# Order of the eight experts in a mixture-of-experts stage, few-row and many-row experts placed differently

## What is computed

```
logits = (tokens @ router_w)
top_vals, top_idx = lax.top_k(logits, 2)
gates = softmax(top_vals)
# for each of the 8 experts e, over the tokens routed to it:
y = (silu(xb @ w1[e]) * (xb @ w3[e])) @ w2[e]      # 1024 -> 2816 -> 1024
out[token] += gate * y
```

## Time and profile before

| what | value |
|---|---|
| median of 3 runs | 2088.28 us (2087.71 to 2107.45) |
| the profiled execution's own time | 2087.27 us |
| its span, first to last instruction | 2084.3 us |
| TensorE matmul busy | 1908.1 us (92%) |
| VectorE, ScalarE busy | 830.7 us (40%), 393.8 us (19%) |
| weight stream | 450 loads of 1 MB, 6.9 us median from issue to landing |

### The profile page before, as it was taken

The page is one execution under the profiler, slowest core; times in us unless marked ns, Lnnn a source line. Parts: engine busy times, 40 slices in busy tenths (PEclk is TensorE's granted clock), DMA queues, the critical chain, the costliest instruction groups (busy, mean ns, idle before and its releaser), DMA issues. The chain is left out here.

```text
span 2084.3 us, 46584 instructions
## 1 busy us (share of the span) xinstructions
PE 1908.1 (92%) x19815; PEld 1617.2 (78%) x19815; DVE 830.7 (40%) x2260; ACT 393.8 (19%) x1114; POOL 0.5 (0%) x5
## 2 busy tenths in 40 slices
PE   6999897999979886999999999999979998899987
PEld 4677676888878776986989968999757876778766
DVE  3856542777758712011101111010113676126651
ACT  2332332000014131000001000000002233122331
POOL 0000000000000000000000000000000000000000
PEclk8999997999989876999999999999998999899988
DMA  9523241889863121989998999989893412234100
GB/s 391 218 101 121 93 171 67 338 335 350 340 245 123 40 81 55 376 330 420 419 349 340 351 392 419 388 321 384 348 419 122 188 73 81 81 121 162 41 1 20
DMA packets 67922, 480.38 MB, mean 230 GB/s; under 512 B 7424, under 2 KB 9728, under 8 KB 9856
## 3 DMA queue, kind: packets, MB, share of 16 engines
q1 hardware_dynamic: 67712, 477.36, 59.2%
HBM read 476.28 MB, written 1.05 MB: 229 GB/s over the span
## 5 line engine op out<-in xcount | busy, mean ns | idle before, releaser
L441 PE MATMUL PS<-sb_U,sb_ring 128*128 128x256 f32 (+1 forms) x1456 | 371.2, 412 | 19.2 <-PEq L217 12.8
L441 PEld LDWEIGHTS PS<-sb_U,sb_ring 128*128 128x128 f32 x1456 | 279.4, 195 | 96.0 <-issue 60.4
L1612 PE MATMUL PS<-sb_arena,sb_ring 128*64 128x98 f32 x7040 | 305.5, 247 | 10.0 <-issue 7.8
L1612 PEld LDWEIGHTS PS<-sb_arena,sb_ring 128*64 128x64 f32 x7040 | 299.5, 136 | 17.0 <-issue 13.3
L688 PE MATMUL PS<-sb_U,sb_ring 128*128 128x256 f32 x704 | 159.6, 386 | 5.7 <-PEq L217 5.7
L1628 PE MATMUL PS<-sb_arena,sb_ring 128*64 128x98 f32 x3520 | 156.6, 248 | 1.6 <-issue 1.4
L1628 PEld LDWEIGHTS PS<-sb_arena,sb_ring 128*64 128x64 f32 x3520 | 149.8, 137 | 9.6 <-ACT sb_arena L1893 6.6
L441 PE MATMUL PS<-sb_arena 128*64 128x128 f32 (+9 forms) x884 | 149.5, 343 | 7.2 <-DVE sb_arena L652 4.4
L688 PEld LDWEIGHTS PS<-sb_U,sb_ring 128*128 128x128 f32 x704 | 134.2, 193 | 23.9 <-issue 6.0
L1945 DVE TENSOR_TENSOR sb_arena<-PS,sb_arena 128x98 f32<-128x98 f32 x110 | 28.6, 260 | 291.6 <-ACT sb_arena L1837 291.6
L441 PEld LDWEIGHTS PS<-sb_arena 64*128 64x128 f32 (+4 forms) x884 | 106.2, 172 | 43.9 <-issue 25.3
(11 more groups left out here) (331 smaller groups left out, 1720.2 us busy)
## 6 DMA issues: line engine op xcount, KB each, us to landing
sb_ring<-stream SPq DMA_DIRECT2D x450, 1024.0 KB, 6.9
sb_consts<-consts SPq DMA_DIRECT2D x1, 1741.0 KB, 27.0
sb_U<-ctxT SPq DMA_DIRECT2D x1, 1024.0 KB, 6.7
sb_XT<-xT SPq DMA_DIRECT2D x1, 1024.0 KB, 8.5
out<-sb_XT SPq DMA_DIRECT2D x8, 128.0 KB, 2.0
sb_small<-small SPq DMA_DIRECT2D x1, 292.0 KB, 2.8
sb_consts<-consts SPq DMA_DIRECT2D x1, 129.0 KB, 2.7
sb_all_small<-layer_small SPq DMA_DIRECT2D x1, 110.0 KB, 27.1
```

The costliest lines, as they stand in the source:

```text
L441: ins = pe.transpose(o, l, r) if t.turn else pe.matmul(o, l, r, start=s, stop=e)
L1612: ins = pe.matmul(PS[c:c + 64, m % 4, h * T:h * T + n], w[:, h, kt, c:c + 64], src[:, kt, 0:n], start=(kt == 0), stop=(kt == KT - 1))
```

## The change

It replaces the order of the ranks. No instruction is added or removed in kind.

```
-RANK_ORDER = (6, 0, 1, 5, 2, 3, 4)
+RANK_ORDER = (6, 0, 5, 1, 4, 2, 3)
```

## The result

The changed kernel is slower: 2106.9 us median (2091.54 to 2117.04) against 2097.01 us (2085.44 to 2107.45), 22 runs each on the same chips, ratio 1.0055 with a 95% interval of 1.0035 to 1.0074. That is +11.5 us by the ratio, +9.9 by the medians. I had forecast 2090.5 us with a range of 2084.5 to 2097.0, and +2.8 us of change. The range missed the time, and the change is three and a half to four times what I had summed.

The account below looks back on a forecast made before the run. TensorE was taken to bound the large places, with the weight stream backed up by few places. Terms +4.8, -2.5 and +0.5 gave +2.8 us on 2087.27, 2090.1, set to 2090.5 us toward the runs' median; range 2084.5 to 2097.

Parts of the forecast that it names:

- the end of the stage: Step from last addition to next stage, 7.37 us: a quieter stream lets instruction fetches find a short queue, -2.5 us.
- the base: Whole run: counted from the profiled execution's 2087.27 us, going half way to the runs' median, 1.0 us above it.
- Rival 2: End of the stage: it pays nothing, the 7.37 us being branch and barrier; 2092.1 to 2093.8 us, chance 0.20.
- The debt of a few place: Large places behind few ones: working through the stream's backlog, with late instructions, costs about 6.8 us each.
- rival 1 in its first form: Third large place behind a few one: debt shrinks from 6.8 to some 1.1 us; 2084.4 us, both forms' chance 0.20.
- The run of 1088 records: Hidden matmuls of place 6: 46.23 us without a gap, read as instruction fetching hidden beside an idle stream.
- eight pieces of 0.7 us: Hidden tiles of place 5: TensorE's gaps for late instructions, said to make the 5.6 us of excess.
- The eight places: Whole stage: 737.2 us against 732.4, +4.8 us for one more large place behind a few one, bounds +3.5 to +6.5.
- The clock: Half-clock stretch behind the stage: recurs at the same length with more work in it, +0.5 us, bounds 0 and 1.2.
- the layers behind it cost nothing more or less: Layers after the stage: no change, as their first nine chunks land before TensorE asks in both orders.
- Rivals 3 and 4: Few places: ring does not refill, 2113 us, chance 0.04; a few place loses the clock, 2100 us, chance 0.06.

Follow-up runs that it names:

- E8: Kernel before without the second leg of the If (the untaken one for exceeded capacity): 2092.1 us, ratio 0.9985.
- E12: Changed kernel without the second leg of the If (the untaken one for exceeded capacity): 2098.63 us, ratio 0.9995.
- E3: Kernel before, with each chunk load of the expert stage bringing only the first half of the chunk's columns: 2062.79 us, ratio 0.9826.
- E4: Changed kernel, with each chunk load of the expert stage bringing only the first half of the chunk's columns: 2052.09 us, ratio 0.9805.
- E1: Kernel before with its places reordered to L F L F L L L F (L large, F few): 2094.39 us, ratio 1.0008.
- E7: Kernel before with its places reordered to L L L L L F F F (L large, F few): 2109.02 us, ratio 1.0061.
- E2: Kernel before with its places reordered to L F L L F L F L (L large, F few): 2101.44 us, ratio 1.0027.
- E10: Changed kernel with at most three chunk loads under way in the expert stage: 2097.8 us, ratio 1.0029.
- E9: Kernel before with at most three chunk loads under way in the expert stage: 2102.3 us, ratio 1.0031.
- E5: Changed kernel with most matmuls of the large places writing all 128 output columns at once, not two halves of 64: 2290.77 us, ratio 1.0961.

## Why the prediction was right and wrong

In short: the mechanism of the stage was right, the end of the stage was wrong, and the base was too low. The time lies 16.4 us above the forecast. Of these, 9.3 us are the base and 7.1 the change (9.9 us by the medians, 2.8 forecast).

**The base: 9.3 us too low. This step failed.** I counted from 2087.7 us, by one execution of 2087.27 us and a median of three. The kernel before has 2097.01 us over 22 runs, and two of the three were at the low end of its 22 us of spread. The range went down with it. Its row was there to be read: a highest run of 2107.45 us beside 2087.71 had to be in the range.

**The end of the stage: -2.5 us forecast, -0.4 measured. This step failed.** I had read the 7.37 us as a fetch that waits in the stream's queue ("a fetch finds a short queue"), for want of a row of a branch beside a quiet stream, and took the middle. The changed kernel itself has the branch beside a quiet stream, and E8 and E12 show that the branch alone makes the 5 us. Rival 2 was right here, though its time of 2092.1 to 2093.8 us was missed as well. The rule of the Trainium skill on taken branches ("Runtime: NRT & Kernel Launch", "Instruction fetch mechanics") pointed there: it names the fetch of the target and says nothing of other traffic. The instruction pieces in the steps with a branch, and none without, agree with it.

**The debt of a few place: right.** Places 2, 4 and 6 took 105.7, 106.4 and 107.8 us where I had 105.4, 105.4 and 106.2. That it is the backed-up stream is shown by E3 and E4, that it reaches TensorE through late instructions by the pieces on q8. So rival 1 in its first form, a third place without the debt, is refuted by the stretches of the changed kernel. The sentence of the Trainium skill ("Runtime: NRT & Kernel Launch", "Instruction fetch mechanics") that fetching is mostly hidden holds for places without a backlog, such as place 3 of before with TensorE busy for all of its 98.55 us; E1's place 6 and the first places of E7 are exceptions.

Two of my readings were loose. The run of 1088 records that I set "beside an idle stream" has the DMA engines 92% busy; what it lacks is the backlog. And the "eight pieces of 0.7 us" are seven waits of 3.8 us in sum in place 5; the other 1.9 of the 5.7 us are in TensorE's busy time.

**The eight places: +4.8 us forecast, +8.3 in the profile, over my upper bound of 6.5.** This term was too small. In other programs the third debt cost 4.6 us (E12 against E8) and 5.1 us (E2's profile, +4.8 at equal clock), but 9.9 us in E10 against E9. At equal clock the changed kernel as a whole has +9.5. So my price was met twice and missed twice, and that it was met is partly luck: with whole chunks and no limit on the loads, a large place behind a few one took anything from 103.5 to 107.8 us in these profiles. In the changed kernel places 4, 6 and 7 are 1.0, 1.6 and 1.0 us over my sum. In places 4 and 6 it is late instructions, which also occur in the output part there (1.3 and 1.8 us). In place 7 they make 0.2 us of it, and the rest is longer busy time. What decides the number of late pieces (how they fall against the chunks, for one) was not tried by moving the code by some instructions, and stays open.

**The clock: +0.5 us forecast for the stretch behind the stage.** That stretch came as expected (0.50 in both kernels). What I left out was every other stretch. The sentence "the layers behind it cost nothing more or less" was wrong for the profiled pair by 9.2 us. As both values occur with both orders, these 9.2 us are no cost of the change.

**Rivals 3 and 4.** The ring refills behind a single large place: with whole chunks and no limit on the loads, the few places take 74.1 to 75.4 us wherever one large place stands before them, also in E1. E7 shows what it would cost otherwise, 83 and 84 us; my 85 was near. No place of the changed kernel lost the clock.

## What to carry to other kernels

A stage that uses its stream faster than it comes leaves a debt, and the debt is paid by what stands behind it. Put such a stage where nothing asks for much of the stream (here last before another layer, which hides one of three debts), and count how many others stand before a bound stage. Where TensorE waits "at issue" at even distances, look at what landed just before: here it was a piece of instructions in the large places, and in the few places a chunk. And before a change of a few microseconds is forecast, look at the spread of the runs and at the mean clock of each: here 1 us at half clock is 0.44 us of time, and the stretches move from execution to execution.

## What the runs showed that I had not expected

- Two matmuls of 64 output columns beside each other are much faster than one of 128 columns, in float32 with 98 moving columns. In the kernel before 1088 records take 46.23 us, 42.5 ns each; a full-width one counts two records for 128 columns and the two halves count four, 170 ns. In E5 fourteen records of the full width take 1.80 us, 129 ns each, 257 ns for 128 columns:

```profile
1259.04 1.80 PE L1612 MATMUL PS<-sb_arena,sb_ring 128*128 128x98 f32 x14
1260.77 0.39 PE L1615 MATMUL PS<-sb_arena,sb_ring 128*64 128x98 f32 x4
```

- A branch over a long leg of an If costs 4.6 to 5.0 us at the end of a stage, with the DMA engines 27% busy as with them busy throughout.
- TensorE's instructions come on a queue of their own in pieces of 16 KB, about 1.1 us each while the stream is backed up, and a gap ends 1.2 to 1.6 us after its piece has landed. The page's 0.5% for that queue does not show that its lateness costs 16 us of gaps in places 2, 4 and 6 of the changed kernel.
- The part of the program behind the stage takes one of two values 10 us apart, by whether some of its stretches get the full clock, in the same instructions.
- With two loads of 1 MB under way the stream delivers 364 GB/s in a few place of the one profile taken. With three it keeps the DMA engines 97 to 98% busy in the place behind one, as it does without a limit.
